# The turned probabilities read back by ScalarE's queue in the next iteration's first loop, in place of SyncE's

## The reference, cut to what matters

```
for i in range(2):
    proj = x @ w_in[i]                       # q, k, v of 3 attention groups, retention q, k, v, g, two gates
    attn = dilated_window_attention(...)     # 3 groups (strides 1, 4, 16), 8 heads of 128, softmax over keys
    ret  = silu(g) * group_norm(retention(...))        # 4 heads, keys 256, values 512
    m    = (sigmoid(gate_a) * (attn @ w_attn_proj) + sigmoid(gate_r) * (ret @ w_ret_proj)) @ w_out
    x    = layer_norm(alpha * x + m)
    ple  = sigmoid(x @ w_ple_gate) * (p @ w_ple_proj)
    x    = layer_norm(alpha * x + conv_gated_mlp(x) + ple)
```

## Time and profile before

| | |
|---|---|
| median of three runs | 1459.02 us |
| the profiled execution, device time | 1458.79 us |
| its span (first to last instruction) | 1457.0 us |
| PE, PEld busy | 1447.1 (99%), 1270.6 (87%) |
| DVE, ACT, POOL busy | 1048.0 (72%), 770.6 (53%), 57.8 (4%) |
| granted TensorE clock | full, in all 40 slices |
| DMA engines | 9787595775966465556555966857759664665560 (tenths, in 40 slices) |

### The profile page before, as it was taken

One profiled execution on the slowest core, in us unless ns is written; L12 is line 12 of the kernel. 1 busy time (PEld: TensorE's weight loads), 2 busy tenths in 40 slices (PEclk: granted clock), 3 DMA queues, 4 the chain that ended last, 5 costly groups with the idle time before them and its releaser, 6 DMA issues.

```text
span 1457.0 us, 20126 instructions
## 1 busy us (share of the span) xinstructions
PE 1447.1 (99%) x8177; PEld 1270.6 (87%) x8177; DVE 1048.0 (72%) x1189; ACT 770.6 (53%) x813; POOL 57.8 (4%) x46
## 2 busy tenths in 40 slices
PE   9999999999999999999999999999999999999998
PEld 8888889888888888888888888888888888888886
DVE  6786766867665688777866668667677557887777
ACT  5455454554644456666544454545546444576562
POOL 0200000000000020000020000000000000100000
PEclk9999999999999999999999999999999999999999
DMA  9787595775966465556555966857759664665560
GB/s 311 242 196 218 173 251 183 195 219 171 224 216 218 160 230 188 203 185 204 177 170 172 215 221 184 243 177 193 231 173 223 205 219 159 212 222 173 196 235 30
DMA packets 357421, 292.00 MB, mean 200 GB/s; under 512 B 104545, under 2 KB 347745, under 8 KB 356705
## 3 DMA queue, kind: packets, MB, share of 16 engines
q1 hardware_dynamic: 356528, 290.14, 65.6%
q10 hardware_dynamic: 816, 0.79, 0.2%
HBM read 277.27 MB, written 13.63 MB: 200 GB/s over the span
## 4 chain that ended last, share of the span: by engine, by line
PE 98%; DVE 1%; ACT 1%; DMA 0%; issue 0%; DVEq 0%; ACTq 0%
PE bank L1451 25%; PE bank L1442 15%; PE bank L1458 13%; PE bank L1437 8%; PE bank L1419 7%; PE bank L1421 7%; PE bank L1420 7%; PE acc L1419 4%; PE acc L1420 4%; PE acc L1421 4%; PE acc L1616 1%; PE acc L1593 1%; PE bank L1492 1%; PE acc L1589 1%; PE acc L1636 0%; PE acc L1573 0%
## 5 line engine op out<-in xcount | busy, mean ns | idle before, releaser
L829 DVE TENSOR_TENSOR w_lo<-raw,w_hi 128x2048 fp32r<-128x2048 f32 x234 | 535.6, 2290 | 216.1 <-ACT w_hi L466 215.5
L466 ACT ACTIVATE w_hi<-raw 128x2048 fp32r<-128x2048 f32 x241 | 459.5, 1908 | 120.3 <-PE bank L1421 44.5
L1451 PE MATMUL bank<-xT_both,w_hi 128*128 128x512 f32 x1472 | 351.1, 391 | 0.0
L1451 PEld LDWEIGHTS bank<-xT_both,w_hi 128*128 128x128 f32 x1472 | 273.9, 188 | 56.0 <-DVE mid_lo L1100 0.4
L1458 PEld LDWEIGHTS bank<-xT_both,w_lo 128*128 128x128 f32 x1472 | 188.7, 191 | 7.2
L1458 PE MATMUL bank<-xT_both,w_lo 128*128 128x256 f32 x1472 | 190.9, 283 | 0.0
L1442 PE MATMUL bank<-xT_both,w_hi 128*128 128x512 f32 x736 | 175.6, 391 | 0.0
L579 ACT ACTIVATE scratch<-bank 128x512 f32<-128x512 f32 x80 | 47.6, 596 | 231.5 <-PE bank L1458 134.9
L1442 PEld LDWEIGHTS bank<-xT_both,w_hi 128*128 128x128 f32 x736 | 135.3, 188 | 26.2
L1421 PE MATMUL bank<-w_hi,xT_both 128*128 128x512 f32 (+1 forms) x400 | 135.6, 339 | 0.0
L1419 PE MATMUL bank<-w_hi,xT_both 128*128 128x256 f32 (+1 forms) x368 | 123.8, 336 | 0.4 <-DVE xT_both L897 0.3
(11 more groups left out here) (185 smaller groups left out, 1688.1 us busy)
## 6 DMA issues: line engine op xcount, KB each, us to landing
raw<-w_in SPq DMA_DIRECT2D x133, 1024.0 KB, 5.1
raw<-w_up SPq DMA_DIRECT2D x44, 1024.0 KB, 5.1
raw<-w_down SPq DMA_DIRECT2D x20, 1024.0 KB, 5.1
raw<-w_ret_proj SPq DMA_DIRECT2D x16, 1024.0 KB, 5.4
prob_blocks<-scratch SPq DMA_DIRECT2D x16, 512.0 KB, 3.2
scratch<-prob_blocks SPq DMA_DIRECT2D x64, 128.0 KB, 4.6
raw<-w_attn_proj SPq DMA_DIRECT2D x8, 1024.0 KB, 5.7
raw<-w_out SPq DMA_DIRECT2D x8, 1024.0 KB, 5.2
```

What stands on the lines that cost most here:

```text
L466: nc.scalar.activation(w_hi[:, s, :], raw[:, s, :], ACT.Copy).then_inc(hi_ready, 1)
L829: nc.vector.tensor_tensor(w_lo[:, s, :], raw[:, s, :], w_hi[:, s, :].bitcast(F32), ALU.subtract).then_inc(lo_ready, 1)
L1451: mm(pair[p][:, m, :], hi[:, o:o + P], src[:, k0 + k, :, :].rearrange("p a t -> p (a t)"), start=first and k == 0, stop=False, skip_group_ ...
```

## The change

`prob_in` is taken out of SP's stream. ACT issues the same eight reads in its loop 0, behind `gates_silu` and ahead of `copy_out` of chunk 0 (mixer iterations 1 to 3) or ahead of the first `gate_low` (merge). The waits are the same (`prob_written[a]`, once ahead of each head's four reads), and so are the semaphores that the reads raise (`probT_in[a]`), the addresses and the sizes.

```diff
-            def prob_in(a, it):
-                sp.wait_ge(prob_written[a], 16 * (it + 1))
-                blocks_in(prob_flat[a], prob_blocks[a, :, :, :], probT_in[a])
...
-                if c == 2:
-                    prob_in(0, it)
-                    prob_in(1, it)
...
+            def prob_in(it):
+
+                for a in range(2):
+                    act.wait_ge(prob_written[a], 16 * (it + 1))
+                    for n in range(4):
+                        v = slice(n * 32, (n + 1) * 32)
+                        act.dma_start(prob_flat[a][v, :].rearrange("p (b r) -> p b r", r=32),
+                                      prob_blocks[a, :, :, v].rearrange("b (i p) r -> p (b i) r", p=32))\
+                          .then_inc(probT_in[a], 16)
...
                     if j and c == 0:
                         gates_silu(l, j)
+                        prob_in(it - 1)
...
                     if c == 0:
                         gates_silu(l, NJ)
+                        prob_in((l + 1) * NJ - 1)
                         gate_low(c0, 0, 0)
```

## The result

The changed kernel takes 1474.61 us (median of three runs, 1474.26 to 1475.06) against 1459.02: 15.6 us more, a ratio of 1.0109 with a 95% interval of 1.0095 to 1.0123. I had forecast 1461.0, with 1466 as the upper end. The place that I named was right, the size was not.

A forecast was written before the change was run, and what follows sets the result against it. PE was taken to bound the kernel, running without a gap. The profiled run's 1458.79 us plus 2.0 for two merge stalls, nothing for mixer iterations or sooner loads, gave 1460.8, or 1461.0 on the median's scale; range 1458.5 to 1466.

The forecast's parts named there:

- What bounds the kernel: PE throughout, busy 1447.1 of 1457.0 us: sooner loads gain next to nothing, any lateness of PE is added in full.
- Where it bites, and the budget of 5.9 us: Two merges: the issues may hold ACT 5.9 us before PE waits for bank pair 0; forecast stall 1.0 us each.
- When the issues begin: On ACT in the merge: at the silu's start, 380.66; the other bound was its end, 1.06 us later.
- my own sign of being wrong: Forecast counted as wrong if, among other signs, the eight issues begin well before the silu.
- How long they take: Eight issues on ACT: 6.9 us, from 5.9 for two measured halves plus 1.0 for SP's competing reads.
- the uncontested sum: Eight issues on ACT without competition: first four 2.31 us, last four 3.57 us, together 5.9 us.
- the company: SP's four retention reads in the merge, 2.3 us of pace, about half falling on ACT's issues: +1.0 us.
- rival 1: All hidden: issues take no more than 5.9 us, time stays 1459.0 us; chance 0.22, shared with a change without effect.
- Rival 2: Merges: ACT held longer, for example 9 us, PE loses 3.1 us in each, 1465.2 us; chance 0.35 for 1462 and up.
- The mixer iterations: Six iterations: issues from 101.18 to 108.1 hidden behind PE's work on chunks 1 and 2; cost nothing.
- a room of 9.7: Mixer iterations: the issues would have to take 9.7 us before PE noticed, at chunk 3.
- My 4.4 us from issue to landing: Median time for a probability read to land after issue; last one lands at 392.0 in the merge, 112.5 in the mixer.

The follow-up runs named there:

- The copies: Kernel before, reads still on SP, with constant copies on ACT ahead of each merge's `gate_low`: four 1458.60 us, seven 1466.78 us, nine 1474.34 us.

## Why the prediction was wrong

**What bounds the kernel.** Right: PE without a gap, no gain from loads that land sooner, any lateness added in full. The transfers that SP could start sooner gave nothing in any run.

**Where it bites, and the budget of 5.9 us.** Right in place and size. The wait stands at the product with `ret`, released by DVE's sum, twice. The copies bear it out. Counted from the start of the silu, as the budget is, four of them held `gate_low` back for 5.3 us and cost nothing; seven held it back for 8.6 us, 2.7 over the budget, and PE waited 2.59 us in each merge.

**When the issues begin.** Right, a little early even: 380.19, just ahead of the silu's start at 380.31, not behind its end. The trace agrees with the rule of the Trainium skill that I had set beside it ("Perfetto Trace Analysis", section "DVE / Act Engine Instruction"). In the mixer iterations they begin earlier still, 1.05 us ahead of the silu in iteration 1 (99.78 against 100.83), beside the table load; that is nearer to my own sign of being wrong, and it cost nothing.

**How long they take: this is the term that failed.** "about half of that falls on ACT before its last issue: +1.0". I took 6.9 us for the issues; they took 11.2 and 10.9. Of the 4.3 us that are missing in the first merge, 1.1 lie in the uncontested sum: without company the issues took 7.0 and 6.6 us, where it had been 5.9 (the first four 2.6 us for my 2.31, the last four 4.4 for my 3.57). The other 3.2 lie in the company: the retention write and reads cost 4.2 us, not 1.0. I left the write out, and I counted the reads at SP's issuing pace in a mixer iteration (2.3 us for four). The earlier trace rows already had 3.98 us for the same four reads in that very merge (the second layer's took 2.56). What ACT waits for is, as I read it, the DMA engines, and there 128-byte packets go at one pace for both queues together. Two windows of the DMA view, of the kernel before with SP's queue alone (372 to 377 us), and of the changed kernel with both (384 to 392 us):

```profile
DMA packets 5684, 0.72 MB, mean 143 GB/s; under 512 B 5684, under 2 KB 5684, under 8 KB 5684
```

```profile
DMA packets 8912, 1.15 MB, mean 144 GB/s; under 512 B 8899, under 2 KB 8911, under 8 KB 8911
...
q10 hardware_dynamic: 4793, 0.60, 81.9%
q1 hardware_dynamic: 4118, 0.53, 73.1%
```

1137 packets per us from one queue, 1114 from two: the second queue adds nothing and takes about half. ACT's last reads therefore went at about half pace as long as SP had anything to move. The rule of the Trainium skill that I had put with rival 1 ("DMA: Bandwidth & Descriptors", section "Issuing engines are not separate DMA queues") says that starting DMAs on several engines saves only the time of initiating them, and these rows agree. It calls this time "usually small relative to the DMA itself"; here it was 11 us on the engine that mattered, and the measurement decides.

**What a stand of PE costs: the term that was missing.** I priced a late PE at its lateness. The profile prices it at 1.5 times that, since the clock falls while PE stands and 2.7 us are paid behind each stand. The kernel before shows no stand in the middle of the program (its longest wait, 1.6 us, lies in the first 60 us), so it showed no price either; I should have named the clock as an unknown.

**The rival.** Rival 2 (ACT held about 9 us, PE loses what exceeds 5.9) was the true one, and its mechanism, transfers that two queues share, is the one that the runs support. Its own arithmetic with the measured durations gives (11.2 - 5.9) + (10.9 - 5.9) = 10.3 us, against 10.24 measured in stands; the clock adds 5.4. I gave it 0.35 and let the range end at 1466, on the ground that SP's 8.8 us came from the load ahead in its queue. That ground was sound as far as it went (7.0 us with nothing beside), and something worse stood in its place.

**The mixer iterations.** Right for the changed kernel: free, with 7.8 to 8.9 us of issues against a room of 9.7. The room was tighter than I said at `attend`: with 10.2 us of issues in iteration 1 the wait came there, 0.8 us, and not at chunk 3. My 4.4 us from issue to landing was the other weak figure: it was the median of SP's reads, and in the merges of the changed kernel the longest took 13.0.

## What to carry to other kernels

Before DMA issues move to a compute engine, ask how long that engine may be held at that place, and price the issues at the pace at which the queues together drain, not at the pace of an empty queue: here eight small-packet DMAs held their issuer for 7.0 us alone, and the other queue's transfers at that moment added 4.2. Where PE never waits, look at what a stand does to the clock: here stands of about 5 us cost half as much again, and one of two waits of 2.6 us did. And when the first wait is taken away and nothing gains, look for the second one close behind it before giving up the mechanism.

## What the runs showed of the hardware that I had not expected

- Two queues with 128-byte packets share one rate: 1114 packets per us together, 1137 alone. Beside packets of 1 KB the share of the small ones swings, and for most of the time it is far under half. In the changed kernel, 393 to 395 us, with a weight load on q1 and the last probability reads on q10:

```profile
q1 hardware_dynamic: 637, 0.65, 104.8%
q10 hardware_dynamic: 54, 0.01, 5.5%
```

  In the next 2 us q10 moved 944 packets and q1 320, and from 397 to 402 us q10 was down to some 16 to 31 per us. So most of the data was through by 397, and the rest trickled; that goes with reads that took up to 13.0 us from issue to landing there, where the longest was 6.7 before. Why the small packets get so few turns stays open.
- Two waits of PE of the same length, 2.59 us, behind the same work: one kept the clock at 2.4 GHz, the other lost it and paid 1.6 us more. Waits of 2.47 and 2.15 us, in the run with the retention reads held back, kept it.
- An ACT sequence runs a DMA issue beside its own activation (380.19 and 380.31 above), but the next activation behind a held issue waits for it; ACT's idle time there reads 10.09 us.
